# Attention values with the value blocks stationary: two heads in two column groups, the turned probabilities moving, heads written turned

## What is computed

```python
def causal_block_attention(q, k, v, log_forget=None):          # groups A and B
    def one_block(i):                                          # 128 queries at a time
        s = jnp.einsum('bqhd,bkhd->bhqk', qi, k, preferred_element_type=jnp.float32) * scale
        ...
        p = jax.nn.softmax(s, axis=-1)
        return jnp.einsum('bhqk,bkhd->bqhd', p.astype(v.dtype), v)
...
    merged = jnp.concatenate([out_a, out_b, out_c, out_d], axis=-1)
    return jnp.einsum('bsm,md->bsd', merged, w_out)
```

## Time and profile before

| | us |
|---|---|
| median of three runs (1075.06 to 1081.79) | 1080.05 |
| the profiled execution | 1074.64 |
| its span | 1072.8 |
| PE busy, share of the span | 988.1, 92% |
| DVE busy | 586.5, 55% |
| ACT busy | 313.8, 29% |
| POOL busy | 90.0, 8% |
| mean granted TensorE clock | 0.971 of full speed |

### The profile page before, as it was taken

The page is one execution under the profiler, slowest core; times in us unless marked ns, Lnnn a source line. Parts: engine busy times, 40 slices in busy tenths (PEclk is TensorE's granted clock), DMA queues, the critical chain, the costliest instruction groups (busy, mean ns, idle before and its releaser), DMA issues.

```text
span 1072.8 us, 13167 instructions
## 1 busy us (share of the span) xinstructions
PE 988.1 (92%) x4871; PEld 620.4 (58%) x4871; DVE 586.5 (55%) x1364; ACT 313.8 (29%) x781; POOL 90.0 (8%) x83
## 2 busy tenths in 40 slices
PE   3799899999999789998989979999999988899986
PEld 0444365689755647666644435568884555667572
DVE  1349799867655633223283778996762254323316
ACT  3131124556321212112142122436652121212103
POOL 3001003000000011000240010210000000101002
PEclk8899999999999899999989989999999998999989
DMA  9985616500475889999936281140006058999946
GB/s 369 306 284 173 235 59 219 236 2 2 145 260 155 282 297 367 384 381 389 313 143 244 65 328 60 42 157 2 1 20 236 20 182 307 355 387 375 388 162 235
DMA packets 138791, 229.69 MB, mean 214 GB/s; under 512 B 31060, under 2 KB 111428, under 8 KB 132428
## 3 DMA queue, kind: packets, MB, share of 16 engines
q1 hardware_dynamic: 129800, 196.34, 52.3%
q0 software_dynamic: 5760, 20.97, 5.3%
q10 hardware_dynamic: 3168, 11.54, 2.7%
HBM read 210.97 MB, written 22.54 MB: 218 GB/s over the span
## 4 chain that ended last, share of the span: by engine, by line
PE 68%; DVE 10%; DMA 9%; SPq 7%; issue 3%; ACT 2%; POOL 0%; ACTq 0%; DVEq 0%; POOLq 0%
PE bank L1265 61%; PE bank L1282 5%; SPq L1846 4%; DMA shared<-in_w_up 4%; DMA wbuf<-in_w_ada 2%; SPq L1850 2%; DMA bada<-in_b_ada 2%; DVE tring L853 1%; DVE shared L789 1%; DVE small L852 1%; ACT shared L546 1%; PE bank L1573 1%; DMA y_rows<-tok 1%; SPq L1762 1%; DVE x L1218 1%
## 5 line engine op out<-in xcount | busy, mean ns | idle before, releaser
L1265 PE MATMUL bank<-shared,wbuf 128*128 128x512 f32 (+2 forms) x640 | 243.4, 539 | 10.3 <-ACT pring L574 9.5
L1265 PE MATMUL bank<-shared 128*128 128x128 f32 (+4 forms) x1248 | 218.7, 332 | 13.2 <-DMA shared<-in_w_up 6.5
L1265 PE MATMUL bank<-wbuf,shared 128*128 128x512 f32 (+3 forms) x672 | 198.4, 494 | 4.4 <-ACT shared L654 3.0
L1265 PEld LDWEIGHTS bank<-shared,wbuf 128*128 128x128 f32 (+1 forms) x640 | 111.4, 192 | 137.2 <-issue 120.1
L1265 PEld LDWEIGHTS bank<-shared 128*128 128x128 f32 (+1 forms) x1248 | 152.6, 191 | 38.6 <-issue 27.1
L1265 PEld LDWEIGHTS bank<-wbuf,shared 128*128 128x128 f32 (+1 forms) x672 | 100.4, 178 | 82.0 <-issue 73.1
L1265 PEld LDWEIGHTS bank<-shared,pring 128*128 128x128 f32 (+1 forms) x640 | 87.0, 187 | 30.2 <-issue 18.7
L1157 DVE TENSOR_TENSOR tring<-bank,tring 128x256 f32<-128x256 f32 x22 | 9.3, 425 | 162.8 <-ACT tring L694 162.8
L1265 PE MATMUL bank<-shared,pring 128*128 128x64 f32 (+1 forms) x640 | 95.1, 290 | 0.9 <-ACT pring L701 0.9
L546 ACT ACTIVATE shared<-bank 64x512 f32<-64x512 f32 (+3 forms) x86 | 48.7, 569 | 133.1 <-PE bank L1265 114.7
L636 ACT ACTIVATE tring<-tring,small 128x384 f32<-128x384 f32 (+5 forms) x128 | 69.3, 541 | 51.5 <-DVE small L926 50.1
(11 more groups left out here) (245 smaller groups left out, 1003.5 us busy)
## 6 DMA issues: line engine op xcount, KB each, us to landing
wbuf<-in_w_ada SPq DMA_DIRECT2D x36, 1024.0 KB, 6.1
shared<-in_w_gate SPq DMA_DIRECT2D x20, 1024.0 KB, 12.9
shared<-in_w_up SPq DMA_DIRECT2D x20, 1024.0 KB, 15.5
shared<-in_w_down SPq DMA_DIRECT2D x20, 1024.0 KB, 14.5
shared<-in_w_ada SPq DMA_DIRECT2D x12, 1024.0 KB, 10.7
wbuf<-in_w_in SPq DMA_DIRECT2D x8, 1536.0 KB, 6.4
wbuf<-in_w_gate SPq DMA_DIRECT2D x12, 1024.0 KB, 12.2
wbuf<-in_w_up SPq DMA_DIRECT2D x12, 1024.0 KB, 14.1
```

The costliest lines, as they stand in the source:

```text
L1265: return nc.tensor.matmul(dst, lhsT, rhs, start=first, stop=last)
```

## The change

The operands of the values change places, and two heads are worked on side by side in the array.

- `pair_values(u)` replaces `unit_values`: for two heads u, u+1 and each key tile, two matmuls, the value block (128 keys x 64) stationary and the turned probabilities (128 keys x 128 queries) moving. One head writes PSUM partitions 0 to 63, the other 64 to 127. The result is the head's output turned, features by queries. It is called at even u for units u-2 and u-1.
- The turned probabilities lie in a ring of four (`turned_probs`, in `tok`).
- 1/sum now stands along the free dimension. DVE inverts the four sums first thing in iteration u where u % 4 == 0 (`invert_sums`); POOL copies them spread over 64 columns each (`spread_sums`, 128 x 256); PE turns that in two transposes, R(og) (`unit_inverse`), in a bank of the ring; ACT drains it into `inverse`; DVE multiplies the output bank with it straight into `hT` (`drain_values`), one iteration later.
- The 32 transposes of `tok`, their 8 drains and the waits around them are gone. `out(i, ...)` waits only for the product of block i of group D.

In the diff, cut:

```diff
@@ plan
+        if u % HEADS == 0 and u > 0:
+            jobs += [(("R", u // HEADS - 1), "act")]
+    jobs += [(("R", n // HEADS - 1), "act")]
-    jobs += [(("mT", k), "act" if k % 2 else "dve") for k in range(KT)]
@@ gpsimd
+                wait_filled(pool, ("vB", 1))
+                for og in range(len(UNITS) // HEADS):
+                    need(pool, sums_inverted, og + 1)
+                    if og >= 2:
+                        wait_filled(pool, ("R", og - 2))
+                    nc.gpsimd.tensor_copy(spread_sums[:, og % 2, :, :], rsd[og % 2].unsqueeze(2).to_broadcast([P, HEADS, HD]))\
+                        .then_inc(sums_spread, 1)
@@ scalar
+                def spread_inverse(og):
+                    if og >= 2:
+                        need(act, o_drained, og - 1)
+                    drain(("R", og), (inverse[:, og % 2, :], bank(("R", og))[:, 0:2 * P]))
...
                     if u + 3 < len(UNITS):
                         exps(u + 3)
-                for k in range(1, KT, 2):
-                    drain(("mT", k), (hT[:, k, :], bank(("mT", k))[:, :]))
+                    if u % HEADS == 0 and u > 0:
+                        spread_inverse(u // HEADS - 1)
+                spread_inverse(last_unit // HEADS)
@@ vector
+                def invert_sums(og):
+                    need(dve, probs_ready, HEADS * (og + 1))
+                    if og >= 2:
+                        wait_filled(dve, ("R", og - 2))
+                    nc.vector.reciprocal(rsd[og % 2], sums[:, og * HEADS:(og + 1) * HEADS]).then_inc(sums_inverted, 1)
+
+                def drain_values(og):
+                    g, i, _ = UNITS[og * HEADS]
+                    k, b = 2 * GROUPS.index(g), banks[6 + og % 2]
+                    need(dve, o_filled, og + 1)
+                    wait_drained(dve, ("R", og))
+                    nc.vector.tensor_tensor(hT[:, k:k + 2, i * P:(i + 1) * P], b[:, 0:2 * P].rearrange("p (c n) -> p c n", c=2),
+                                            inverse[:, og % 2, :].rearrange("p (c n) -> p c n", c=2), ALU.mult).then_inc(o_drained, 1)
+
                 for u in range(len(UNITS)):
+                    if u % HEADS == 0 and u > 0:
+                        invert_sums(u // HEADS - 1)
                     if u % 2 == 0:
...
-                    if u % HEADS == 0 and u > 0 or u == last_unit:
...
+                    if u % HEADS == 1 and u > 1:
+                        drain_values(u // HEADS - 1)
+                invert_sums(last_unit // HEADS)
+                drain_values(last_unit // HEADS)
@@ tensor
-                def unit_values(u):
+                def pair_values(u):
...
-                    for t in range(n // P):
-                        last = mm(banks[6 + og % 2][:, h * HD:(h + 1) * HD], pring[:, u % 3, t * P:(t + 1) * P],
-                                  V[g](h, k0 // P + t), t == 0, t == n // P - 1)
-                    if h == HEADS - 1:
+                    for t in range(n // P):
+                        for side in range(2):
+                            last = mm(b[HD * side:HD * (side + 1), at:at + P], V[g](h + side, k0 // P + t),
+                                      turned_probs[:, (u + side) % 4, t * P:(t + 1) * P], t == 0, t == n // P - 1)
+                    if h == 2:
                         last.then_inc(o_filled, 1)
+
+                def unit_inverse(og):
+                    need(pe, sums_spread, og + 1)
+                    b = bank(("R", og))
+                    turn(("R", og), [(b[:, c * P:(c + 1) * P],
+                                      spread_sums[:, og % 2, 2 * c:2 * c + 2, :].rearrange("p h n -> p (h n)"), P) for c in range(2)])
...
-                    if u > 0:
-                        unit_values(u - 1)
-                unit_values(last_unit)
-
-                need(pe, o_drained, len(UNITS) // HEADS)
-                for k in range(KT):
-                    turn_rows(("mT", k), k)
+                    if u % HEADS == 0 and u > 0:
+                        unit_inverse(u // HEADS - 1)
+                    if u % 2 == 0 and u > 0:
+                        pair_values(u - 2)
+                unit_inverse(last_unit // HEADS)
+                pair_values(last_unit - 1)
...
-                wait_drained(pe, ("mT", KT - 1))
-                wait_drained(pe, ("mT", KT - 2))
                 need(pe, wout_landed, 16)
                 for i in range(TT):
+                    need(pe, o_drained, (len(GROUPS) - 1) * TT + i + 1)
```

More of the change, by code:

```diff
@@ L231, in trunk @@
     onec = small[:, 50:51]
-    rsd = small[:, 52:56]
+    rsd = [small[:, 52:56], small[:, 98:102]]
     max8 = small[:, 56:64]
@@ L269, in trunk @@
     score = tring[:, 0, :]
+    inverse = latent[:, 4 * SEQ:5 * SEQ].rearrange("p (a n) -> p a n", a=2)
+    spread_sums = latent[:, 5 * SEQ:6 * SEQ].rearrange("p (a h n) -> p a h n", a=2, h=HEADS)
+    turned_probs = latent[:, 0:4 * SEQ].rearrange("p (a n) -> p a n", a=4)
     relu = [pring[:, 0, :], pring[:, 1, :], pring[:, 2, :]]
@@ L332, in trunk @@
     probs_ready = sem("probs_ready")
+    sums_inverted, sums_spread = sem("sums_inverted"), sem("sums_spread")
     o_filled, o_drained = sem("o_filled"), sem("o_drained")
@@ L430, in trunk @@
               forget_ready: 2, forget_landed: 8 * 16, softplus_ready: 1,
-              probs_ready: len(UNITS), o_filled: len(UNITS) // HEADS, o_drained: len(UNITS) // HEADS,
+              probs_ready: len(UNITS), o_filled: len(UNITS) // HEADS, sums_inverted: len(UNITS) // HEADS,
+              sums_spread: len(UNITS) // HEADS, o_drained: len(UNITS) // HEADS,
               diag_ready: 2, wrs_ready: 1, shift_ready: 1, logits_ready: TT, scores_ready: 1, x_added: 2 * TT, gates_ready: 1, rows2_ready: TT,
@@ L643, in _ @@
                         n = keys(*UNITS[u][:2])[1]
-                        drain(("T", u), (pring[:, u % 3, 0:n], bank(("T", u))[:, 0:n]))
+                        drain(("T", u), (turned_probs[:, u % 4, 0:n], bank(("T", u))[:, 0:n]))
                     if u + 3 < len(UNITS):
                         exps(u + 3)
-                for k in range(1, KT, 2):
-                    drain(("mT", k), (hT[:, k, :], bank(("mT", k))[:, :]))
+                    if u % HEADS == 0 and u > 0:
+                        spread_inverse(u // HEADS - 1)
+                spread_inverse(last_unit // HEADS)
                 def spread(name):
@@ L937, in _ @@
                         wait_filled(dve, ("T", u))
-                        nc.vector.tensor_copy(pring[:, u % 3, 0:n], bank(("T", u))[:, 0:n]).then_inc(dve_drained, 1)
+                        nc.vector.tensor_copy(turned_probs[:, u % 4, 0:n], bank(("T", u))[:, 0:n]).then_inc(dve_drained, 1)
                     if u + 3 < len(UNITS):
                         scores(u + 3)
-                    if u % HEADS == 0 and u > 0 or u == last_unit:
[L942 to L948, removed]
-                                banks[6 + og % 2][:, 0:256].rearrange("p (h d) -> p h d", h=HEADS),
-                                rsd.unsqueeze(2).to_broadcast([P, HEADS, HD]), ALU.mult).then_inc(o_drained, 1)
-                for k in range(0, KT, 2):
-                    wait_filled(dve, ("mT", k))
-                    nc.vector.tensor_copy(hT[:, k, :], bank(("mT", k))[:, :]).then_inc(dve_drained, 1)
+                    if u % HEADS == 1 and u > 1:
+                        drain_values(u // HEADS - 1)
+                invert_sums(last_unit // HEADS)
+                drain_values(last_unit // HEADS)
                 def diagonals(n, v):
```

4 lines of the change are left out of this document (3 added, 1 removed).

## The result

| | before | after |
|---|---|---|
| median, us | 1078.03 (four runs, 1075.06 to 1081.79) | 1091.44 (four runs, 1086.69 to 1094.79) |
| ratio, with its 95% interval | | 1.0112 [1.0078, 1.0147] |
| the profiled execution, and its span | 1074.64, 1072.8 | 1092.35, 1090.4 |
| mean granted TensorE clock | 0.971 | 0.964 |

The change makes the kernel 1.1% slower: 1091.44 where 1095 was predicted, +13.4 where +15 was. (The median of before is 1078.03 with a fourth run, 1076.01; the prediction counted from 1080.05, the median of three.) Line 1293 is now the matmul helper, 1310 the turns, 494 POOL's copy, 561 ACT's drain, 810 the modulation step.

A forecast was written before the change was run, and what follows sets the result against it. PE was taken to bound the kernel nearly everywhere. Layer 0 at 0.6 + 9.8 - 0.6 = +9.8 and layer 1 at 0.6 + 9.8 - 5.05 = +5.3 gave +15 on 1080.05: 1095 us, range 1070 to 1114.

The forecast's parts named there:

- The values: Value matmuls in the unit loop, run in pairs: 17.1 us a layer instead of 29.4, bounds 15.8 and 18.4.
- The change of shape: Switching PE's array into two column groups and back: 0.29 us both ways, 32 times a layer, 9.3 us.
- R on PE and the wait: In the unit loop, each layer: 32 transposes, 3.6 us, and PE waiting for POOL's copy at 15 R, 9.8 us.
- The loop: First turn to last value record, each layer: 10.55 us longer, with 0.6 of PE work and 9.8 of waiting.
- The tail: Last value record to projection, each layer: 5.2 us shorter; in layer 0, 4.4 us come back as waits.
- No overlap of the column groups: Rival, values: each record takes 0.107 us alone, 31.7 us for 17.1; +29 more, 1124 us; chance 0.04.
- shape changes free: Rival, around the values: changing the array's shape costs nothing between short matmuls; -3.6, 1076 us; chance 0.14.
- R ready: Rival, unit loop: R is ready when PE comes, so no wait; -4.6, 1075 us; chance 0.08.
- POOL stretched by DVE: Rival, POOL's copy before R: a busy DVE stretches it to 1.27 us; +24, 1119 us; chance 0.09.
- The best case: Rival, unit loop: values take half their time, shape changes cost nothing, R does not wait; -23, 1057 us; chance 0.09.

The follow-up runs named there:

- the wide copy: The changed kernel with POOL's copy twice as wide, 512 columns instead of 256, the second half used: 1096.46 us, one execution.
- the earlier blocks: The changed kernel with layer 0's two next modulation blocks loaded behind the first expert instead of the second: 1085.26 us, 1.0070 of before.
- four-units kernel: The changed kernel with R one iteration later and, on top, values of four units together every fourth iteration: 1066.26 us, 0.9893 of before.
- the later R: The changed kernel with R's transposes, their drain on ACT and DVE's product each one iteration later: 1073.81 us, 0.9974 of before.
- sides apart: The changed kernel with the values' loops exchanged, all key tiles of one head first, then the other's: 1098.83 us, one execution.

## Why the prediction was right, step by step

**The values.** Right in kind, and at the low end in size. The two records of a pair start 6 or 7 ns apart (36 ns where the block stood behind a wait), and the next pair 0.109 us after the one before, so 148 pairs take 16.1 us; the bounds were 15.8 and 18.4, I took 17.1. The smallest step of 0.06 us per record that I had found in the small transposes does not bound this: two records start in 0.109.

**The change of shape.** Right. In the trace after, the matmul behind a block starts 0.210 after the last pair instead of 0.109, and the next transpose 0.164 after it instead of 0.109: 0.156. Into the block, the first value record comes 0.094 late and the second pair 0.160 after the first instead of 0.109: 0.145. The sum is 0.30, for 0.29 in the prediction, and the experiment with half the changes gives 0.29. The rule of the Trainium skill, TensorEngine Tiling (Array Packing), Key Properties, that a change of tiling mode drains TensorE, agrees with these rows, also between matmuls as short as these. Its advice to swap the operands and tile the columns twofold, When to Use Tiling, holds here for the records alone (two in 0.109 us). It does not hold for the loop, where the ways in and out cost 0.30 us each time.

**R on PE and the wait.** The mechanism was right in every link, the size 10% too large: over the 15 R of a layer the wait is 8.9 us (steps from score record to R 11.94, less 3.9 that they would take unhindered, plus 0.055 for each second transpose), 9.8 predicted. The mis-sized term is POOL's copy: 0.402 us, not 0.46, 15 x 0.06 = 0.9. I had put it halfway between a memset and a product of two inputs, and it lies nearer the memset. The estimate of 0.38 that I had worked out from the Trainium skill, GPSIMD Engine Reference, section 3.1, was nearer than my middle, but by luck. At its 1.8 cycles an element 256 more elements would take 0.38 us more, and the wide copy took 0.211 more; the other 0.19 of the 0.402 is a fixed part, which that estimate left out. By number of tiles of the next group the step to R exceeds the unhindered one by 0.78 to 0.84 at one tile, 0.59 to 0.68 at two, 0.40 at three and 0.21 at four, and 0.05 more for the second transpose; predicted 0.90, 0.76, 0.52, 0.31.

**The loop.** +10.55 predicted, +8.7 seen. Of the 1.8, the values near their low bound are 1.0 and the copy 0.9; against them stands a wait of 0.4 that I had missed; 0.3 is left over, spread over many small steps. The values of units 60 and 61 wait for ACT's drain of T(61) too, not only those of the last pair: [0.34 <-ACT tok L561] at 291.42, which makes that step 0.614 instead of 0.20.

**The tail.** 5.2 us, as predicted, in both layers. (The prediction's terms, 281.48 + 0.14 + 0.86 + 0.15, give 282.63 and not the 282.7 it went on with, so its own gain was 5.13.) In layer 1 it stays. In layer 0 I expected 4.4 of it to come back as waits: 3.2 did. The modulation step starts 317.30 - 294.70 = 22.6 us behind the last value record, where it was 306.14 - 282.36 = 23.8; the loads were 1.2 us quicker than in the profile of before. I had taken their time as fixed. The traces point to why: 16 KB of instructions (DMA queue q8) are fetched at 287.82 in before, 5.5 us behind the last value record, for 1.12 us in the middle of the loads, and the second expert block lands 10.1 us behind that record. In after they are fetched at 295.02, 0.3 us behind it, before the loads have begun, and that block lands at 8.9. It is so in all ten traces: late fetch and 10.0 to 10.1 us in the two kernels with the old end of the loop, early fetch and 8.9 to 9.1 in the eight others. But no run moved the fetch alone, so this cause is not shown.

**What was not in the sum.** Behind these two waits the granted clock fell, and the same matmuls took twice as long for a few microseconds. Windows of PE in the kernel after (clock is the third number from the right):

```profile
322.00:330.00 8.00, 6.76 (x16) 1.00 0.48 176
...
331.90:333.90 2.00, 2.00 (x5) 0.50 0.82 328
...
334.00:340.00 6.00, 6.00 (x14) 0.91 0.42 130
```

The records at 321.93 to 322.79 of before step by 0.43, those at 333.31 to 335.02 of after by 0.86: that is the clock at 0.50, 1.2 GHz for 2.4. It costs 1.7 us up to there, and a pause inside the router product before it 0.2. Another 2 us come from later falls, at other places than before's. Then there are the 3.6 us ahead of the first loop, where the code is the same. Of these, 3.2 arise between 114 and 128 us: DVE waited 1.75 us for a modulation block instead of 0.14, PE behind it 5.90 instead of 3.98, and the clock was then at 0.50 for 6.8 us instead of 3.4. The kernel with the wide copy has 0.11 and 3.73 for these two waits, so I put them down to the spread between executions. With all this taken off, 17.7 becomes 10.2: the loops' 17.5 less 10.4 of tails, and 3.2 of waits. The medians say 13.4, so the two profiled executions lie some 4 us too far apart, and the 3 us between 10.2 and 13.4 are perhaps the clock falls, which is argued and not shown; that the earlier blocks give this kernel 3.0 us more than the waits they remove speaks for it. The forecast of +15 was too large by 2 x 1.8 in the loops and 1.2 at the loads, and had nothing for the clock; part of its nearness is that these partly cancel.

**The rivals.** No overlap of the column groups falls by the pairs; shape changes free, by the four-units kernel; R ready, by the waits in the trace and by the later R, which takes them away; POOL stretched by DVE, by 16 copies of 0.395 to 0.404 us, 15 of them beside a busy DVE and the last, 0.403, beside an idle one. The best case, values at half and no wait, was not a rival of this kernel but a neighbour of it: four units at once with R later comes to 1066, and to 1060 with the loads moved.

## What to carry to other kernels

A cheaper form of an operation brings a price for every switch into and out of it: count the switches (here 32 a layer at 0.30 us ate 9.6 of the 29.4 - 16.1 = 13.3 us that the shorter matmuls gave), and batch the work between them before judging the form. When a result goes through three engines before PE can use it, put its use one iteration later than it seems ready; that alone was worth 17 us here. And a stretch that becomes shorter moves the wait to the next transfer that was released ahead of it: ask for each layer separately what lands last, since a reorder of loads that was worth nothing before can be worth 4 to 6 us after.

## What was unexpected in the hardware

- By my reading of their starts, matmuls in two column groups overlap even if written one group after the other, over the last four records of the first group: eight records (four and four) start in pairs 0.014 us apart throughout; in sixteen (eight and eight) the first four and the last four go alone at 0.109 us.
- A short wait inside a busy stretch can cost more than itself. Over the ten microseconds behind the router product of layer 0 the granted clock was 0.83, 0.66 and 0.83 in three of the five kernels in which PE had waited twice just ahead (after, the wide copy, four units with the old loads), 1.00 in the other two (later R, sides apart), and 1.00 in all five in which it had not waited. After with the blocks earlier shows it at another place: behind waits of 1.06 and 0.62 us just ahead of the first loop its clock fell to 0.50 for 3.4 us, where waits of 0.9 and 0.65 left it at 1.00 in the nine other traces. Each is one execution, so this is a pattern and not yet a rule; what decides between the two outcomes stays open.
- POOL's broadcast copy of one column into 64 took 0.402 us for 128x256 and 0.613 for 128x512: 0.19 us and 0.82 ns for each element of a partition, and a busy DVE beside it did not stretch it (0.395 to 0.404 us in 16 copies).
